# Dense borders by token block, and the loop over two layers written out

## The chip, the cores and the metric

The kernel runs on one core of one Trainium2 chip. The metric is the device time of one execution in microseconds (us); the times given are the median of three runs with their extremes. All inputs and the output are in HBM; the host does no arithmetic.

## The reference

An activation x of 256 tokens by 1024 features (f32) goes through two blocks. The first has two layers, each a mixer (a convolution mixer, then a linear recurrence), a layer norm, a mixture of 16 experts with two chosen per token, and a layer norm. The second, the dense part, has two layers of

```
h = h + 0.5 * swiglu(rms_norm(h, ffn1_norm), w_gate, w_up, w_down)       # 1024 -> 2816 -> 1024
h = h + hybrid_mixer(rms_norm(h, mix_norm), w_in, ..., w_out)           # 1024 -> 3792, attention, 1024 -> 1024
h = h + 0.5 * swiglu(rms_norm(h, ffn2_norm), w_gate, w_up, w_down)
rms_norm(x, g) = x * rsqrt(mean(x*x) + 1e-6) * g
```

The hybrid mixer splits its projection into three kinds of attention (chosen keys, one block, forgetting) with normalised and rotated heads.

## The kernel before

**Layout.** x lies in SBUF as [128 partitions, TB=2 token blocks, 1024]. `xT_hi` and `xT_lo` hold it transposed, [128, KC=8 feature chunks, 256 tokens], cut into a rounded fp32r part and its remainder. Every product of the dense part is made of three fp32r matmuls, hi*hi, hi*lo and lo*hi (`exact`, L1583; `exact_w`, L1891). PSUM has eight banks of 512 f32: `acc` (four: block 0 in banks 0 and 1, block 1 in 2 and 3) collects what is added to x, `W` (four) everything else.

**Weights** come as numbered chunks of up to 128x2048 f32 (1 MB). SyncE's queue loads chunk c into one of six `raw` slots (`load`, L404) once the slot's last chunk has its remainder. ScalarE rounds it to `w_hi` (`split`, L625, one ACTIVATE at L633), VectorE subtracts to `w_lo` (`rest`, L974, one TENSOR_TENSOR at L977); there are three split slots. TensorE waits for `lo_ready` of the chunk and counts `used` when it is done; `split(c)` waits for `used` of chunk c-3. Splits and rests stand in the engines' own order of instructions, written by hand, AHEAD = 3 chunks before TensorE needs them.

**An FFN** (TensorE L1878, ScalarE L864, VectorE L1346) has eleven groups of 256 hidden columns with three chunks each: gate and up (`up`: weights stationary, `xT` moving, 256 tokens wide, 48 matmuls a chunk, into a bank of `W`) and down (`into_acc`, L1610: hidden values stationary, 512 weight columns moving, 24 matmuls a chunk). The groups overlap: gate and up of the next group run before down of this one; an inner loop runs over most groups.

**The mixer** begins with a projection of 16 half chunks (`projection`, L1589: `xT` of a block stationary, 474 weight columns moving, 24 matmuls a chunk, bank by block); its sums are evacuated to `proj`, block 0 by ScalarE (L897), block 1 by VectorE. It ends with `out_projection` (eight chunks of 12 matmuls into `acc`).

**A border** between two stages is: `add_to_x` on VectorE (L1334) waits for the last chunk's `used`, adds `acc` to x for both blocks and signals `x_ready`. `rms` (ScalarE L850, VectorE L1325): ScalarE squares block 0 with a sum, VectorE block 1, ScalarE takes the root of both (L856), VectorE the reciprocal, and each writes its block normalised to `xn` (L858, L1332). `transposes` (TensorE, L1559): eight 128x128 transposes of block 0, then of block 1, into `W`, two feature chunks of both blocks to a bank. `transposed` (ScalarE L643, VectorE L997): eight ACTIVATEs of 128x256 with the norm's gain write `xT_hi`, eight SCALAR_TENSOR_TENSORs write `xT_lo`. VectorE issues the rests of the next chunks between `rms` and `transposed`. Then TensorE starts on the first chunk, waiting pair by pair for `xT_lo` (`wait_xT`).

The dense part stands in a loop over the two layers on every engine (`Fori(0, DEPTH)`, L524, L604, L952, L1535, L2010), so the layer's gain columns and semaphore counts are taken from registers. After it SyncE stores x whole (L534).

## Time and profile before

| | us |
|---|---|
| median of 3 runs (lowest, highest) | 2483.45 (2482.26, 2487.23) |
| the profiled execution | 2489.44 |
| its span, first to last instruction | 2487.8 |
| TensorE busy | 2232.2 (90%) |
| VectorE busy | 955.8 (38%) |
| ScalarE busy | 719.6 (29%) |
| mean granted TensorE clock | 0.942 |

Engines are called PE (TensorE matmul), PEld (TensorE weight load), DVE (VectorE), ACT (ScalarE), POOL (GpSimd), SP (SyncE); a q behind the name is the engine's sequencer or DMA queue. L12 is line 12 of the kernel. Matmuls are pipelined: the duration of one is longer than the distance at which they follow one another, and it is the distance of two starts that tells the pace. The dense part begins at 1233.8 us of the span.

### The profile page before, as it was taken

How to read it: one execution, taken by the hardware profiler on the slowest of the kernel's cores; microseconds unless marked ns; L12 is line 12 of the kernel's file. 1: busy time of each engine (PE TensorE's matmuls, PEld its weight loads, DVE VectorE, ACT ScalarE, POOL GpSimd, SP SyncE). 2: the span in 40 equal slices, each digit the busy share in tenths (PEclk: the TensorE clock that was granted, in tenths of full speed). 3: DMA queues.
4: the chain of work that ended last, by engine and by line, in shares of the span. 5: the costliest groups of instructions: out<-in, count | busy, mean ns of one | idle time of the engine just before them, and what ended most of it. 6: DMA issues, size and time to landing. Idle time of an engine off the chain costs nothing.

```text
span 2487.8 us, 30159 instructions
## 1 busy us (share of the span) xinstructions
PE 2232.2 (90%) x12373; PEld 1559.5 (63%) x12373; DVE 955.8 (38%) x1217; ACT 719.6 (29%) x896; POOL 68.1 (3%) x78
## 2 busy tenths in 40 slices
PE   8869999997866999999599987979989998897998
PEld 6544334332754343333299976769979997676998
DVE  4741000001673000000345557645545546754554
ACT  4621000001451000000333344243343334424332
POOL 2000000000000000000100010000000001000000
PEclk9979999999987999999899989789999999968999
DMA  7189999999439999999955542045545554304551
GB/s 258 37 361 423 425 424 424 423 425 417 163 126 383 425 424 424 424 424 425 333 190 185 177 133 94 1 139 186 185 136 187 186 178 141 101 1 136 176 183 64
DMA packets 194676, 618.56 MB, mean 249 GB/s; under 512 B 10360, under 2 KB 119040, under 8 KB 145408
## 3 DMA queue, kind: packets, MB, share of 16 engines
q1 hardware_dynamic: 192416, 612.01, 64.6%
q0 software_dynamic: 2144, 4.94, 0.8%
q8 instruction: 81, 1.33, 0.2%
q14 instruction: 35, 0.29, 0.0%
HBM read 615.86 MB, written 1.05 MB: 248 GB/s over the span
## 4 chain that ended last, share of the span: by engine, by line
PE 72%; DMA 12%; DVE 8%; ACT 3%; DVEq 2%; issue 2%; ACTq 0%; SPq 0%
PE W L1730 18%; PE W L1892 7%; PE W L1893 7%; PE W L1894 7%; DMA moe_own<-in_moe_w 5%; DMA moe_split<-in_moe_w 5%; PE acc L1620 4%; PE acc L1621 4%; PE acc L1624 4%; PE W L1585 4%; PE W L1586 4%; PE W L1587 4%; PE W L1714 2%; DMA moe_xt<-in_moe_w 2%; PE acc L1723 2%
## 5 line engine op out<-in xcount | busy, mean ns | idle before, releaser
L977 DVE TENSOR_TENSOR w_lo<-raw,w_hi 128x2048 fp32r<-128x2048 f32 (+2 forms) x216 | 466.6, 2163 | 473.4 <-ACT w_hi L633 472.0
L633 ACT ACTIVATE w_hi<-raw 128x2048 fp32r<-128x2048 f32 (+2 forms) x216 | 382.3, 1772 | 595.6 <-PE W L1894 320.6
L1892 PE MATMUL W<-xT_hi,w_hi 128*128 128x256 f32 x1408 | 401.2, 285 | 7.5 <-DVE xT_lo L997 7.5
L1893 PE MATMUL W<-xT_lo,w_hi 128*128 128x256 f32 x1408 | 400.6, 285 | 0.0
L1894 PE MATMUL W<-xT_hi,w_lo 128*128 128x256 f32 x1408 | 400.5, 284 | 0.0
L1228 DVE TENSOR_TENSOR hid<-W,hid 128x512 f32<-128x512 f32 x32 | 22.1, 692 | 735.6 <-PE W L1730 735.6
L1892 PEld LDWEIGHTS W<-xT_hi,w_hi 128*128 128x128 f32 x1408 | 270.2, 192 | 10.3 <-DVE xT_lo L997 8.9
L1893 PEld LDWEIGHTS W<-xT_lo,w_hi 128*128 128x128 f32 x1408 | 270.2, 192 | 1.6
L1894 PEld LDWEIGHTS W<-xT_hi,w_lo 128*128 128x128 f32 x1408 | 270.3, 192 | 0.0
L1585 PE MATMUL W<-w_hi,xT_hi 128*128 128x474 f32 (+1 forms) x400 | 155.3, 388 | 9.9 <-DVE w_lo L977 4.8
L1730 PE MATMUL W<-moe_split,xe 128*64 128x512 f32 x672 | 153.2, 597 | 9.5 <-DMA moe_split<-in_moe_w 8.2
L1586 PE MATMUL W<-w_lo,xT_hi 128*128 128x474 f32 (+1 forms) x400 | 155.3, 388 | 0.0
L1587 PE MATMUL W<-w_hi,xT_lo 128*128 128x474 f32 (+1 forms) x400 | 154.5, 386 | 0.0
L1730 PE MATMUL W<-moe_own,xe 128*64 128x512 f32 x608 | 138.1, 596 | 6.0 <-DMA moe_own<-in_moe_w 5.9
L1620 PE MATMUL acc<-w_hi,hT_hi 128*128 128x512 f32 x352 | 138.3, 393 | 1.7 <-DVEq L1358 1.7
L1730 PE MATMUL W<-raw,xe 128*64 128x512 f32 x576 | 132.1, 597 | 6.9 <-DMA raw<-in_moe_w 6.6
L1621 PE MATMUL acc<-w_lo,hT_hi 128*128 128x512 f32 x352 | 137.7, 391 | 0.0
L1730 PEld LDWEIGHTS W<-moe_split,xe 128*64 128x64 f32 x672 | 45.8, 137 | 112.0 <-issue 90.9
L1624 PE MATMUL acc<-w_hi,hT_lo 128*128 128x512 f32 x352 | 109.3, 392 | 0.0
L1730 PEld LDWEIGHTS W<-moe_own,xe 128*64 128x64 f32 x608 | 41.5, 137 | 99.0 <-issue 77.4
L756 ACT ACTIVATE xe<-W 128x512 f32<-128x512 f32 x32 | 19.1, 597 | 278.3 <-PE W L1714 278.3
L1730 PEld LDWEIGHTS W<-raw,xe 128*64 128x64 f32 x576 | 39.0, 136 | 96.3 <-issue 77.0
(334 smaller groups left out, 2743.9 us busy)
## 6 DMA issues: line engine op xcount, KB each, us to landing
moe_own<-in_moe_w SPq DMA_DIRECT2D x120, 1024.0 KB, 26.2
moe_split<-in_moe_w SPq DMA_DIRECT2D x120, 1024.0 KB, 26.2
raw<-in_moe_w SPq DMA_DIRECT2D x108, 1024.0 KB, 25.8
raw<-in_ffn_w_gate SPq DMA_DIRECT2D x44, 1024.0 KB, 5.3
raw<-in_ffn_w_up SPq DMA_DIRECT2D x44, 1024.0 KB, 5.3
raw<-in_ffn_w_down SPq DMA_DIRECT2D x44, 1024.0 KB, 4.9
moe_xt<-in_moe_w SPq DMA_DIRECT2D x36, 1024.0 KB, 26.0
raw<-in_w_in SPq DMA_DIRECT2D x32, 948.0 KB, 4.9
```

The source lines that it names most:

```text
L633: s.activation(w_hi[split_slot(c)][:, 0:cols], raw[slot_of(c)][:, 0:cols], ACT.Copy).then_inc(hi_ready, 1)
L977: v.tensor_tensor(w_lo[split_slot(c)][:, 0:cols], raw[slot_of(c)][:, 0:cols], w_hi[split_slot(c)][:, 0:cols].bitcast(F32), ALU.subtract).t ...
L1585: t.matmul(out, a_hi, b_hi, start=first, stop=False)
L1586: t.matmul(out, a_hi, b_lo, start=False, stop=False)
L1587: return t.matmul(out, a_lo, b_hi, start=False, stop=last)
L1620: t.matmul(acc[:, 2 * b + n, :], a_hi(k)[:, tok], hi[:, cols], start=st, stop=False)
L1621: t.matmul(acc[:, 2 * b + n, :], a_hi(k)[:, tok], lo[:, cols], start=False, stop=False)
L1624: last = t.matmul(acc[:, 2 * b + n, :], a_lo(k)[:, tok], hi[:, cols], start=False, stop=sp_)
L1730: last = t.matmul(W[CAP * n:CAP * (n + 1), bank, :], stationary[:, kc, :], weights[:, at0 + 512 * n:at0 + 512 * (n + 1)], start=(kc == 0), ...
L1892: t.matmul(out, hi, xT_hi[:, kc, :], start=(kc == 0), stop=False)
L1893: t.matmul(out, hi, xT_lo[:, kc, :], start=False, stop=False)
L1894: return t.matmul(out, lo, xT_hi[:, kc, :], start=False, stop=(kc == KC - 1))
```

## The change

- The three dense loops are written out in Python: addresses and counts are constants. The test for a crowded expert in SyncE's queue stands in layer 0 alone.
- The last chunk into `acc` is computed block by block and signals `acc0` when block 0 is complete. VectorE adds block 0 then (`add_first`), block 1 after the chunk, in two halves (`add_second`).
- Transposes are by block and go to separate banks: block 0 to `W`, block 1 to `acc` (`turned_block`). Copies and remainders are 128 tokens wide, sixteen of each a border.
- Before the mixer x is transposed without its normalisation, which is put as a scale on the evacuations of the projection; block 0's transposes stand inside the last down chunk, block 1's inside the projection's first chunk, whose two halves are computed by block.
- Before an FFN `rms` goes by block, and the two first chunks are computed by block, 128 tokens wide (`up_block`).
- Splits and rests of the next chunks stand at other places around the borders. The output is stored in two halves.

The core of the diff ("..." where lines are left out):

```diff
+        def turned_block(b, kc):
+
+            return (W, acc)[b][:, kc // 2, P * (kc % 2):P * (kc % 2 + 1)]
@@ sync
+            rows_out = out.rearrange("a (b p) d -> p (a b) d", p=P)
+            sp.wait_ge(rm["x0"], 1 + 3 * DEPTH)
+            sp.dma_start(rows_out[:, 0, :], x[:, 0, :]).then_inc(stored, 16)
             sp.wait_ge(x_ready, X_LAYERS + 3 * DEPTH)
-
-            sp.dma_start(out.rearrange("a (b p) d -> p (a b) d", p=P), x[:]).then_inc(stored, 16)
-            sp.wait_ge(stored, 16)
+            sp.dma_start(rows_out[:, 1, :], x[:, 1, :]).then_inc(stored, 16)
+            sp.wait_ge(stored, 32)
 
@@ scalar
+            def turned(call, gain, b, pairs=range(4)):
+
+                for q in pairs:
+                    act.wait_ge(xt_ps, turned_already(call) + 4 * b + q + 1)
+                    for kc in (2 * q, 2 * q + 1):
+                        last = s.activation(xT_hi[:, kc, b * P:(b + 1) * P], turned_block(b, kc), ACT.Copy, scale=gain(kc))
                     last.then_inc(xt_hi_s, 1)
...
+            def rms(call, at0, gain):
+
+                own = slice(0, 512)
+                s.activation(std[:, 0:1], onec[:], ACT.Sqrt)
+                act.wait_ge(rm["x0"], (call + 1).v)
+                s.activation(xn[:, 0, own], x[:, 0, own], ACT.Square, scale=D ** -0.5, accum_out=squares[:, 0:1])
+                act.drain()
+                act.wait_ge(rm["ssd"], at0.times(2).v + 1)
+                s.activation(std[:, 0:1], squares[:, 0:1], ACT.Sqrt, bias=squares[:, 1:2]).then_inc(rm["std"], 1)
+                act.wait_ge(rm["rs"], root_count(call))
+                s.activation(xn[:, 0, :], x[:, 0, :], ACT.Copy, scale=rstd[:, 0:1]).then_inc(rm["xa"], 1)
+                act.wait_ge(rm["x1a"], (call + 1).v)
+                s.activation(xn[:, 1, own], x[:, 1, own], ACT.Square, scale=D ** -0.5, accum_out=squares[:, 2:3])
+                act.drain()
+                xt = N(4 + 4 * (call.base // 3) + (0, 1, 3)[call.base % 3])
+                turned(xt, gain, 0, range(2))
+                act.wait_ge(rm["ssd"], at0.times(2).v + 2)
+                s.activation(std[:, 1:2], squares[:, 2:3], ACT.Sqrt, bias=squares[:, 3:4]).then_inc(rm["std"], 1)
+                turned(xt, gain, 0, range(2, 4))
+                turned(xt, gain, 1)
+
+            def mean_squares(call):
 
                 act.wait_ge(x_ready, (call + X_LAYERS).v)
-                s.activation(xn[:, 0, :], x[:, 0, :], ACT.Square, accum_out=std[:, 0:1])
-                act.drain().then_inc(rm["ssa"], 1)
-                act.wait_ge(rm["ssd"], (call + 1).v)
-                s.activation(std[:], std[:], ACT.Sqrt, bias=rmeps[:], scale=1.0 / D).then_inc(rm["std"], 1)
-                act.wait_ge(rm["rs"], (call + 1).v)
-                s.activation(xn[:, 0, :], x[:, 0, :], ACT.Copy, scale=rstd[:, 0:1]).then_inc(rm["xa"], 1)
...
@@ scalar, mixer
+                        act.wait_ge(rm["rs"], root_count(N(1, (l, 3))))
                     s.activation(proj[:, 0, IN_COLS * j:IN_COLS * (j + 1)], W[:, (2 * j) % 4, 0:IN_COLS],
-                                 ACT.Copy).then_inc(tm_act, 1)
+                                 ACT.Copy, scale=rstd[:, 0:1]).then_inc(tm_act, 1)
...
@@ scalar, loop
-            with act.Fori(0, DEPTH) as l:
+            for l in range(DEPTH):
                 c0 = N(C_LAYERS).plus(l, LAYER_CHUNKS)
-                rms(N(0, (l, 3)))
-                transposed(N(4, (l, 4)), gain_of("ffn1_norm_2", l))
+                rms(N(0, (l, 3)), N(0, (l, 2)), gain_of("ffn1_norm_2", l))
+                split(c0 + (AHEAD - 1))
                 ffn(c0 + C_FFN1, False)
-                rms(N(1, (l, 3)))
-                transposed(N(5, (l, 4)), gain_of("mix_norm_2", l))
+                for b in range(TB):
+                    turned(N(5, (l, 4)), gain_of("mix_norm_2", l), b)
+                split(c0 + (C_FFN1 + FF_CHUNKS - 1 + AHEAD))
+                mean_squares(N(1, (l, 3)))
                 mixer(l, c0)
-                rms(N(2, (l, 3)))
-                transposed(N(7, (l, 4)), gain_of("ffn2_norm_2", l))
+                rms(N(2, (l, 3)), N(1, (l, 2)), gain_of("ffn2_norm_2", l))
+                split(c0 + (C_MIX_OUT + KC - 1 + AHEAD))
                 ffn(c0 + C_FFN2, True)
-                with act.If(l < DEPTH - 1):
-                    for k in range(AHEAD):
+                if l < DEPTH - 1:
+                    for k in range(AHEAD - 1):
...
@@ vector
+            def add_first(call, scale):
+
+                dve.wait_ge(rm["acc0"], call.v)
+                v.scalar_tensor_tensor(x[:, 0, :], acc[:, 0:2, :].rearrange("p a n -> p (a n)"), scale, x[:, 0, :], ALU.mult, ALU.add)
+                v.drain().then_inc(rm["x0"], 1)
+
+            def add_second(count, scale):
+
+                dve.wait_ge(used, count.v)
+                v.scalar_tensor_tensor(x[:, 1, 0:512], acc[:, 2, :], scale, x[:, 1, 0:512], ALU.mult, ALU.add)
+                v.drain().then_inc(rm["x1a"], 1)
+                v.scalar_tensor_tensor(x[:, 1, 512:], acc[:, 3, :], scale, x[:, 1, 512:], ALU.mult, ALU.add)
+                v.drain().then_inc(x_ready, 1)
+            def square_half(b):
+                v.tensor_tensor_reduce(xn[:, b, 512:], x[:, b, 512:], x[:, b, 512:], 1.0 / D, RMS_EPS, ALU.mult, ALU.add,
+                                       squares[:, 2 * b + 1:2 * b + 2])
                 v.drain().then_inc(rm["ssd"], 1)
-                dve.wait_ge(rm["std"], (call + 1).v)
-                v.reciprocal(rstd[:], std[:])
+
+            def reciprocal_root(count, blocks):
+                dve.wait_ge(rm["std"], count)
+                v.reciprocal(rstd[:, blocks], std[:, blocks])
                 v.drain().then_inc(rm["rs"], 1)
+
+            def rms(call, gain, second=None, between=None):
+
+                if second is None:
+                    dve.wait_ge(x_ready, (call + X_LAYERS).v)
+                square_half(0)
+                reciprocal_root(root_count(call), slice(0, 1))
+                if second is not None:
+                    second()
+                square_half(1)
+                xt = N(4 + 4 * (call.base // 3) + (0, 1, 3)[call.base % 3])
+                turned(xt, gain, 0, range(1))
+                reciprocal_root(root_count(call) + 1, slice(1, 2))
                 v.tensor_scalar(xn[:, 1, :], x[:, 1, :], rstd[:, 1:2], None, ALU.mult).then_inc(rm["xd"], 1)
...
+                if between is not None:
+                    between()
+                turned(xt, gain, 0, range(1, 4))
+                turned(xt, gain, 1)
...
@@ vector, loop
-            with dve.Fori(0, DEPTH) as l:
+
+            for l in range(DEPTH):
                 c0 = N(C_LAYERS).plus(l, LAYER_CHUNKS)
-                rms(N(0, (l, 3)))
-                rest(c0)
+                if l == 0:
+                    rms(N(0), gain_of("ffn1_norm_2", l), between=lambda: rest(c0))
                 rest(c0 + 1)
-                transposed(N(4, (l, 4)), gain_of("ffn1_norm_2", l))
                 rest(c0 + 2)
                 ffn(c0 + C_FFN1, N(0, (l, 2 * FF_GROUPS)), False)
-                rms(N(1, (l, 3)))
+
+                add_first(N(1, (l, 3)), 0.5)
+                turned(N(5, (l, 4)), gain_of("mix_norm_2", l), 0)
+                add_second(c0 + (C_FFN1 + FF_CHUNKS), 0.5)
+                turned(N(5, (l, 4)), gain_of("mix_norm_2", l), 1)
                 rest(c0 + (C_FFN1 + FF_CHUNKS - 1 + AHEAD))
-                transposed(N(5, (l, 4)), gain_of("mix_norm_2", l))
+                reciprocal_root(root_count(N(1, (l, 3))), slice(0, TB))
                 mixer(l, c0)
-                rms(N(2, (l, 3)))
+
+                add_first(N(2, (l, 3)), 1.0)
+                rms(N(2, (l, 3)), gain_of("ffn2_norm_2", l), lambda: add_second(c0 + (C_MIX_OUT + KC), 1.0))
+                rest(c0 + (C_MIX_OUT + KC - 2 + AHEAD))
                 rest(c0 + (C_MIX_OUT + KC - 1 + AHEAD))
-                transposed(N(7, (l, 4)), gain_of("ffn2_norm_2", l))
                 ffn(c0 + C_FFN2, N(FF_GROUPS, (l, 2 * FF_GROUPS)), True)
+
+                if l < DEPTH - 1:
+                    rest(c0 + LAYER_CHUNKS)
+                add_first(N(3, (l, 3)), 0.5)
+                if l < DEPTH - 1:
+                    rms(N(3, (l, 3)), gain_of("ffn1_norm_2", l + 1), lambda: add_second(c0 + LAYER_CHUNKS, 0.5))
+                else:
+                    add_second(c0 + LAYER_CHUNKS, 0.5)
 
 
...
@@ tensor
+            def turn_block(call, b, src, ready):
+
+                pe.wait_ge(*ready)
+                for q in range(4):
+                    for kc in (2 * q, 2 * q + 1):
+                        last = t.transpose(turned_block(b, kc), src[:, b, kc * P:(kc + 1) * P], ident[:])
+                    last.then_inc(xt_ps, 1)
+
+            def wait_block(call, b, kc):
+                if kc % 2 == 0:
+                    pe.wait_ge(xt_lo_s, turned_already(call) + 4 * b + kc // 2 + 1)
...
+                if second is not None:
+                    def block(half, b):
+                        c = c0 + half
+                        pe.wait_ge(lo_ready, (c + 1).v)
+                        hi, lo = w_hi[split_slot(c)], w_lo[split_slot(c)]
+                        for k in range(4):
+                            kc = 4 * half + k
+                            wait_block(call, b, kc)
+                            tok = slice(b * P, (b + 1) * P)
+                            last = exact(W[:, b, 0:n], xT_hi[:, kc, tok], xT_lo[:, kc, tok],
+                                         hi[:, k * n:(k + 1) * n], lo[:, k * n:(k + 1) * n], kc == 0, kc == KC - 1)
+                        return last
+
+                    block(0, 0)
+                    second()
+                    block(1, 0)
+                    block(0, 1).then_inc(used, 1)
+                    block(1, 1).then_inc(used, 1)
+                for j in range(0 if second is None else 1, groups):
                     for half in range(2):
...
+                steps = [(k, b) for b in range(TB) for k in range(kn)] if final else [(k, b) for k in range(kn) for b in range(TB)]
...
+                    if ends and (k, b) == (kn - 1, 0):
+                        last.then_inc(rm["acc0"], 1)
+                    if midway is not None and (k, b) == (0, 1):
+                        midway()
                 last.then_inc(used, 1)
...
+                def up_block(c, bank, b):
+
+                    pe.wait_ge(lo_ready, (c + 1).v)
+                    hi, lo = w_hi[split_slot(c)], w_lo[split_slot(c)]
+                    for f in range(2):
+                        for kc in range(KC):
+                            if f == 0:
+                                wait_block(call, b, kc)
+                            cols = slice(kc * FF_COLS + f * P, kc * FF_COLS + (f + 1) * P)
+                            last = exact_w(W[:, bank, f * SEQ + b * P:f * SEQ + (b + 1) * P], hi[:, cols], lo[:, cols], kc,
+                                           slice(b * P, (b + 1) * P))
+                    return last
+
+                def exact_w(out, hi, lo, kc, tok=slice(0, SEQ)):
...
-                up(c0 + 1, 1)
+                    into_acc(c, 2, lambda k: hT_hi[:, parity, k, :], lambda k: hT_lo[:, parity, k, :], first, final, final, midway)
+
+                turn_block(call, 0, xn, (rm["xa"], norm_count))
+                up_block(c0, 0, 0)
+                turn_block(call, 1, xn, (rm["xd"], norm_count))
+                up_block(c0 + 1, 1, 0)
+                up_block(c0, 0, 1).then_inc(used, 1)
+                up_block(c0 + 1, 1, 1).then_inc(used, 1)
```

## Rows read from the trace of the kernel before

**Rows 1.** The page's chain of work that ended last, shares by engine.
```profile
PE 72%; DMA 12%; DVE 8%; ACT 3%; DVEq 2%; issue 2%; ACTq 0%; SPq 0%
```

**Rows 2.** Timeline of VectorE, FFN1 to mixer, layer 0: start, duration (us), instruction [idle before].
```profile
1433.84 2.35 DVE L1338 SCALAR_TENSOR_TENSOR x<-acc,x 128x1024 f32<-128x1024 f32 x2 [2.38 <-PE acc L1624]
...
1444.45 3.28 DVE L997 SCALAR_TENSOR_TENSOR xT_lo<-W,vecs,xT_hi 128x256 fp32r<-128x256 f32 x8 [1.73 <-ACT xT_hi L643]
```

**Rows 3.** Timeline of ScalarE, the same border.
```profile
1437.85 1.28 ACT L856 ACT_TABLE_LOAD   x1 [0.45 <-issue]
...
1439.70 1.15 ACT L858 ACTIVATE xn<-x,rstd 128x1024 f32<-128x1024 f32 x1 [0.26 <-DVEq L1331]
1443.45 3.03 ACT L643 ACTIVATE xT_hi<-W,vecs 128x256 fp32r<-128x256 f32 x8 [2.60 <-PE W L1564]
```

**Rows 4.** Timeline of TensorE's matmuls, the same border.
```profile
1440.90 3.68 PE L1564 MATMUL W<-ident,xn 128*128 128x128 f32 x16 [7.11 <-ACT xn L858]
1446.21 0.76 PE L1585 MATMUL W<-w_hi,xT_hi 128*128 128x474 f32 x1 [1.63 <-DVE xT_lo L997]
...
1449.14 0.60 PE L1586 MATMUL W<-w_lo,xT_hi 128*128 128x474 f32 x1
...
1451.02 0.38 PE L1587 MATMUL W<-w_hi,xT_lo 128*128 128x474 f32 x1
...
1451.87 0.38 PE L1585 MATMUL W<-w_hi,xT_hi 128*128 128x474 f32 x1
```

**Rows 5.** Timeline of ScalarE: rows at which a border begins or its first chunks end.
```profile
1233.81 1.06 ACT L853 ACTIVATE xn<-x 128x1024 f32<-128x1024 f32 x1 [1.18 <-DVEq L1046]
...
1257.10 1.91 ACT L633 ACTIVATE w_hi<-raw 128x2048 fp32r<-128x2048 f32 x1 [1.94 <-PE W L1894]
...
1654.27 1.91 ACT L633 ACTIVATE w_hi<-raw 128x2048 fp32r<-128x2048 f32 x1 [0.80 <-PE acc L1624]
...
1681.28 1.91 ACT L633 ACTIVATE w_hi<-raw 128x2048 fp32r<-128x2048 f32 x1 [1.93 <-PE W L1894]
...
1883.22 1.91 ACT L633 ACTIVATE w_hi<-raw 128x2048 fp32r<-128x2048 f32 x1 [1.94 <-PE W L1894]
...
2059.95 1.91 ACT L633 ACTIVATE w_hi<-raw 128x2048 fp32r<-128x2048 f32 x1 [4.71 <-PE acc L1624]
...
2082.99 0.57 ACT L897 ACTIVATE proj<-W 128x474 f32<-128x474 f32 x1 [3.40 <-PE W L1587]
...
2305.39 1.91 ACT L633 ACTIVATE w_hi<-raw 128x2048 fp32r<-128x2048 f32 x1 [1.93 <-PE W L1894]
```

**Rows 6.** Timeline of VectorE: mixer to FFN2, then FFN2 to FFN1.
```profile
1653.50 2.29 DVE L977 TENSOR_TENSOR w_lo<-raw,w_hi 128x2048 fp32r<-128x2048 f32 x1 [0.43 <-ACT w_hi L633]
...
1856.89 2.36 DVE L1338 SCALAR_TENSOR_TENSOR x<-acc,x 128x1024 f32<-128x1024 f32 x2 [8.91 <-PE acc L1624]
1862.70 1.22 DVE L1327 CUSTOM_DVE_ANT_0 xn<-x 128x1024 f32<-128x1024 f32 x1 [3.45 <-issue]
```

**Rows 7.** Timeline of all engines: loads and matmuls as an FFN starts.
```profile
1871.40 0.19 PEld L1892 LDWEIGHTS W<-xT_hi,w_hi 128*128 128x128 f32 x1 [2.37 <-DVE xT_lo L997]
...
1871.51 0.19 PEld L1893 LDWEIGHTS W<-xT_lo,w_hi 128*128 128x128 f32 x1
1871.63 0.28 PE L1893 MATMUL W<-xT_lo,w_hi 128*128 128x256 f32 x1
...
1871.98 0.28 PE L1893 MATMUL W<-xT_lo,w_hi 128*128 128x256 f32 x1
```

**Rows 8.** Timeline of weight loads: the router's, 16 columns of fp32r.
```profile
156.23 0.10 PEld L1585 LDWEIGHTS W<-xT_hi,wr_hi 128*16 128x16 f32 x1 [1.19 <-issue]
156.26 0.10 PEld L1586 LDWEIGHTS W<-xT_lo,wr_hi 128*16 128x16 f32 x1
```

**Rows 9.** The chain in order of time: four f32 matmuls of 128 columns.
```profile
1582.44 0.85 PE W L1976 x4
```

**Rows 10.** Timeline: the final store is issued.
```profile
2483.42 0.39 SPq L534 DMA_DIRECT2D out<-x  x1
```

More of the change, by code:

```diff
@@ L110, in __init__ @@
     def __init__(self, base, *terms):
-        self.base, self.terms = base, terms
+        self.base = base + sum(r * k for r, k in terms if isinstance(r, int))
+        self.terms = tuple((r, k) for r, k in terms if not isinstance(r, int))
     def __add__(self, n):
@@ L192, in build_program @@
         std = at("std", [P, TB])
+        squares = at("squares", [P, 4])
         rstd = at("rstd", [P, TB])
@@ L477, in first_after_moe @@
                 def first_after_moe(i):
-                    if which == 1:
+                    if which == 1 and l == 0:
                         sp.wait_ge(moe_used, raw_freed(1, i))
@@ L499, in ffn @@
                     down(c + 2, j)
-                    if j == 0 and which == 1:
-                        more_rounds(1, crowded(sp, 1, l))
+                    if j == 0 and which == 1 and l == 0:
+                        more_rounds(1, crowded(sp, 1))
                     if j == 0:
@@ L672, in layer_norm @@
                 if c_next is not None:
-                    split(N(c_next + 1), after_moe=i // 2)
-                    split(N(c_next + 2), after_moe=i // 2)
+                    for k in range(1, AHEAD - 1 if c_next == C_LAYERS else AHEAD):
+                        split(N(c_next + k), after_moe=i // 2)
             transposed(N(0))
@@ L887, in ffn @@
                             silu(1 - t, c0 + (i + 1))
-                if not last:
-                    split(c0 + (FF_CHUNKS - 1 + AHEAD))
             def mixer(l, c0):
@@ L2007, in mixer @@
                 wait_xT(N(6, (l, 4)))
[L2008 to L2010 removed]
+                out_projection(c0 + C_MIX_OUT, ends=True)
+            for l in range(DEPTH):
                 c0 = N(C_LAYERS).plus(l, LAYER_CHUNKS)
[L2013 to L2018 removed]
+                ffn(c0 + C_FFN1, N(0, (l, 2 * FF_GROUPS)), N(4, (l, 4)), 2 * l + 1,
+                    lambda: turn_block(N(5, (l, 4)), 0, x, (rm["x0"], N(2, (l, 3)).v)))
                 mixer(l, c0)
[L2020 to L2021 removed]
+                ffn(c0 + C_FFN2, N(FF_GROUPS, (l, 2 * FF_GROUPS)), N(7, (l, 4)), 2 * l + 2)
 SMALL_LOADS = 4 + sum(len(names) for names in VEC_SETS)
```

143 lines of the change are left out of this document (65 added, 78 removed).

## The prediction

> **What bounds the kernel now.** I read the chain of waits first. TensorE is 72% of it, DMA 12%, VectorE 8% and ScalarE 3% [rows 1]. The DMA share lies in the mixture of experts, which the change leaves alone; the VectorE and ScalarE share is to be looked for between the dense stages. The timelines of one border (the first FFN's end to the mixer's start, layer 0) show it: addition to x, squares, root, normalisation, 16 transposes, eight gained copies and eight remainders, and TensorE standing from about 1433.8 to 1446.2 but for the transposes [rows 2 to 4]. There are six borders into a norm (norm to FFN1, FFN1 to mixer, mixer to FFN2, FFN2 to FFN1, FFN1 to mixer, mixer to FFN2) and the end. Inside the FFNs TensorE takes each chunk without a pause, so what a border gains or loses reaches the end whole.
>
> To compare, I take for each border the moment E, at which the last product is done, and the moment at which the work that the change reorders (the two first chunks) is used up. ScalarE's rows that wait for that moment give it [rows 5]: norm to FFN1 1233.8 to 1257.1, 23.3 us; mixer to FFN2 1654.3 (its last split starts there) to 1681.3, 27.0 (the second layer's end, 2305.39, is 624 later, as its whole border is); FFN2 to FFN1 1856.9 [rows 6] to 1883.2, 26.3; FFN1 to mixer 2060.0 to 2083.0, 23.0 (in layer 0 TensorE's first eight or so matmuls start 0.4 us apart, later ones 0.2125, (1451.87-1451.02)/4 [rows 4]: half rate, 1.2 for 2.4 GHz, some 1.6 more).
>
> **Borders into the mixer.** The final down product now ends block 0 after 12 of its 24 matmuls, 2.74 us before E. Call that A. VectorE adds block 0 in 1.2 (half of L1338's 2.35 [rows 2]). TensorE has one six-matmul step of block 1 meanwhile, so it waits some 0.5, transposes block 0 (half of 3.68 cold [rows 4], near 1.0 warm by its 16 at half that) and then has the last step, 1.4, as cover. An activation of 128 columns I put at 0.27 us: 256 take 0.38 (3.03/8), 1024 take 1.15 [rows 3]. A remainder of 128 is 0.28 by 3.28/8 and 1.18 [rows 2]. A pair is thus 0.55 on either engine, where it was 0.8; the doubled count costs little. Block 0 is ready at about A+4.7, but its first half, which is all that half a chunk needs, at A+3.6. The products start at A+4.3. Four pieces of 12 matmuls at 0.2125 [rows 4] are 2.6 each. Behind the first piece TensorE waits for x of block 1: VectorE does it after block 0's remainders, two halves of 0.7, at A+6.5, just in time; transposes 1.2; then the second piece covers block 1's copies. End at about A+16, or E+13.3, where it was E+23.0. The moved rest of the third chunk (2.3 [rows 6]) ends near A+13.8 and TensorE asks for it at A+16; mean_squares (two squares, 2.4, and the table load of 1.28 [rows 3]) ends its reciprocal near A+15.9 and is asked for with the first evacuation. Both are hidden; without that cover they would cost about 2 each. The normalisation itself, which was on the path, has gone into the evacuation's scale at no cost. **Gain 9.7 in layer 1, 11.3 in layer 0: 21 us.**
>
> **Borders into an FFN: the price of a matmul of 128 columns.** Here up_block halves the moving columns (256 to 128) and doubles the count: 192 matmuls and 192 weight loads where 96 were. No fp32r matmul of under 256 columns is in the trace. What bounds it? At 1871.40 an empty TensorE starts a load; the next load starts 0.11 later, and the second matmul 0.23 later, the following at 0.117 each [rows 7]. So a load of 128x128 fp32r holds its path for 0.11, and behind it a 256-column matmul for as long again. With weights of 16 columns two loads start 0.03 apart [rows 8]: the 0.11 goes with the number of weight columns, and halving the moving columns doesn't touch it. Bounds: from below 0.060, half of today's spacing, if columns alone set it; from above 0.213, as 128-column matmuls of f32 are spaced (0.85/4) [rows 9], if narrow fp32r falls back to that. I take 0.113, between the 0.11 of a load and the 0.117 at which pairs with the same load run [rows 7], the nearest in kind. Then the two chunks cost 21.7 us of TensorE instead of 11.5: +10.2 at each of four borders.
>
> **What they win.** FFN2 to FFN1, from E: acc0 comes 2.74 before it, x of block 0 at -1.4. Squares of half a row on each engine (half of L1327's 1.22 [rows 6]), root with its table loaded ahead (1.28 hidden [rows 3]), reciprocal: +0.25; the copy of block 0, 1.15: xn0 at +1.5, where the transposes started at +8.9. Writing the loop out also takes away the 3.4 that VectorE stood without a releaser at the turn of the loop [rows 6], all within that 8.9. But then one pair after another comes, held up on VectorE by reciprocal and xn1 (0.17+0.75): the fourth remainder ends at +6.5, the first block's two halves at +10.5, block 1's transposes at +11.6.
>
> **The new wait.** up_block(c0+1, 1, 0) waits for lo_ready of the second chunk. Before, both rests stood ahead of the remainders. Now VectorE issues rest(c0+1) behind all of turned(..., 1), which needs ScalarE's copies of block 1, which need the transposes that TensorE issues just before this wait. In its queue nothing can pass. Last pair +13.9 (four pairs, 2.2, behind the transposes), rest 2.3: TensorE goes on at +16.3, having stood 4.6. Three pieces of 48 at 0.113 follow, 16.3, and signals: +33.3 against 26.3. **Loss 7.** SyncE's loads wait for these rests too, but the FFN asks for a megabyte in 5.8 us and has six slots: hidden.
>
> Mixer to FFN2: block 0 has only a six-matmul lead (1.4), and ScalarE's table load falls after its last split. xn0 at +3.7, fourth remainder +8.7, block 0's piece +12 to 13.5, transposes, stall, +19; pieces and a little half-rate running: +36 against 27. Loss 9, twice. To its credit the rest that delayed the addition (1653.50 to 1655.8 [rows 6]) stands behind it now; that is in these numbers. Norm to FFN1: nothing of x is ready early. The rest of the first chunk, 2.3, is put between xn1 and the remainders, so the fourth is ready at +10.2 after x; +13.6 (warm) to 17.5 (half rate) for the piece, transposes and stall +19.5 to 23, end +36 to 40 against 23.3. Loss 14. **FFN borders: -7-9-9-14 = -39.** Running at half rate after a wait, as the first matmuls of layer 0's mixer do [rows 4], is where these four vary by 2 or 3 each.
>
> **The end.** x of block 1 in halves is ready 0.8 sooner; of the final store (issued 2483.42, the span ends at 2487.8 [rows 10]) half goes ahead, and 0.5 MB at the 2.6 us that 1 MB moves is 1.3 less: 2 us.
>
> **Sum:** 21 + 2 - 39 = 16 us slower. The profiled execution took 2489.4 (span 2487.8), 6.0 above the median of 2483.45; so 2505.5 in its terms and **2499.5** in the median's. Other edits (fixed instead of register addresses, squares, the SyncE test left out) I put at nothing, within 1 either way: they lie beside running matmuls, except that 16 small instructions could be quicker with fixed scalars.
>
> **Rivals.**
> A, the other side: the moving columns set the pace, and the load hides behind the stream before it. Then a matmul takes 0.067 (0.060 and an allowance), and 168 of the 192 at each border (the first 24 wait for remainders anyway) are 0.046 cheaper, 31 us in all: 2468. It decides from a spacing of about 0.09 down. For it: the stream at 256 columns doesn't slow with 128-column weights against 16. Against: the 0.11 between loads [rows 7, 8]. Chance 0.19.
> B: narrow fp32r runs as f32, 0.213 per matmul: 0.1 more on 168 at four borders, 67 us: 2566. Nothing here shows or excludes it. 0.12.
> C: the load spacing holds, but the stall is smaller, since the rest lands before TensorE gets there (it would have to overtake the remainders), or the small copies are quicker: four stalls of 4.6 off: 2481. Against it is the written order. 0.09.
> D: something between A and my value. The Trainium skill, TensorE: Matmul & The Clock Gate, "Back-to-back issue gap", gives load and matmul pairs of 128 columns a sustained 81 ns. By it the 168 would be 0.032 cheaper each, 21.5 us in all, which gives 2478. The trace has no such pair; its loads 0.11 apart speak against it. From rows the same place is the middle of 0.060 and 0.113 (0.087): 2482. Chance 0.07.
>
> **Chances.** My forecast 0.53, its own range 2489 to 2512. Measurement tells this kernel from no change at about 0.2%, 5 us, thus 2478.5 to 2488.4. Faster: A 0.19, half of D 0.04, a third of C 0.03: 0.26. Same: 0.03 of D and 0.05 of C: 0.08. Slower: forecast 0.53, B 0.12, the rest of C: 0.66. The range takes in A and leaves out most of B: 2464 to 2520.
>
> **What would show it.** The distance of two up_block matmuls at full clock: 0.11, 0.065 or 0.21. TensorE's idle before block (c0+1, 0) in each FFN, released by w_lo: 4 to 5 us, four times. At the mixer borders no idle above 1 us, and the time from E to the first evacuation near 13. If the spacing is 0.11 and the total is faster, my reckoning of the gaps is wrong; if the spacing is less, the price was.

## The result: slower by 3.9%, and where it went

The changed kernel takes 2583.11 us (median of four runs, 2582.44 to 2585.31); the kernel before, run beside it, 2485.34. The ratio is 1.0391, with a 95% interval of 1.0372 to 1.0409. The forecast was 2499.5 in a range of 2464 to 2520: the sign was right, the time lies far outside. The profiled execution took 2582.44 with a span of 2580.4, 92.6 more than the span before, and its mean granted clock was 0.920 where it was 0.942.

The chain of waits, answering to [rows 1], and the granted clock in 40 slices, from the page of the changed kernel:

```profile
PEclk9979999998979999999599997969987999887899
...
PE 73%; DMA 13%; DVE 8%; ACT 3%; DVEq 2%; issue 1%; ACTq 0%; SPq 0%
```

The chain's shares say next to nothing: TensorE has a point more. The clock line says more: the dense half, from the 20th digit on, holds a 5, a 6 and three 7s where it held a 6 and a 7, though TensorE's share of busy time has risen to 91%. ScalarE's rows that wait for the moment at which the two first chunks are used up, or for the mixer's first sums, answer to [rows 5]:

```profile
1242.07 0.63 ACT L877 ACTIVATE xn<-x 128x512 f32<-128x512 f32 x1 [4.19 <-DVEq L1092]
...
1297.40 1.91 ACT L653 ACTIVATE w_hi<-raw 128x2048 fp32r<-128x2048 f32 x1 [6.42 <-PE W L2025]
...
1490.36 0.64 ACT L937 ACTIVATE proj<-W,rstd 128x474 f32<-128x474 f32 x1
...
1732.40 1.91 ACT L653 ACTIVATE w_hi<-raw 128x2048 fp32r<-128x2048 f32 x1 [6.42 <-PE W L2025]
...
1960.94 1.91 ACT L653 ACTIVATE w_hi<-raw 128x2048 fp32r<-128x2048 f32 x1 [6.42 <-PE W L2025]
...
2153.30 0.64 ACT L937 ACTIVATE proj<-W,rstd 128x474 f32<-128x474 f32 x1
...
2398.00 1.91 ACT L653 ACTIVATE w_hi<-raw 128x2048 fp32r<-128x2048 f32 x1 [6.42 <-PE W L2025]
```

The difference of neighbouring rows is the length of a stretch; each holds one border and the undisturbed work around it. Set against the same stretches of before (layer 0's first evacuation was at 1458.56 there), in us; the last column is the version with whole chunks of the next section:

| stretch | before | changed | difference | predicted | whole chunks, difference |
|---|---|---|---|---|---|
| up to x ready | 1233.8 | 1242.1 | +8.3 | 0 | +8.7 |
| norm to FFN1 | 23.3 | 55.3 | +32.0 | +14 | +0.7 |
| to the mixer, layer 0 | 201.5 | 193.0 | -8.5 | -11.3 | -10.3 |
| to FFN2, layer 0 | 222.7 | 242.0 | +19.3 | +9 | -10.8 |
| FFN2 to FFN1 | 201.9 | 228.5 | +26.6 | +7 | -6.2 |
| to the mixer, layer 1 | 199.8 | 192.4 | -7.4 | -9.7 | -8.6 |
| to FFN2, layer 1 | 222.4 | 244.7 | +22.3 | +9 | -11.3 |
| to the end | 182.4 | 182.4 | 0.0 | -2 | -1.2 |

In what follows a matmul is narrow with 128 moving columns and wide with 256, and the level is the granted clock: 0.50 is half (1.2 GHz), 1.00 is full (2.4 GHz). The four borders into an FFN cost 100.2, not 39, and something ahead of the dense part costs 8.3. One FFN border in windows (columns: window, its length, busy time and instructions of TensorE, its weight loads, VectorE, ScalarE and GpSimd, granted clock, DMA share, GB/s):

```profile
1250.00:1260.00 10.00, 9.74 (x46) 9.74 (x46) 1.76 (x7) 0.00 (x0) 0.00 (x0) 0.50 0.36 107
1262.00:1266.00 4.00, 0.49 (x3) 0.09 (x1) 4.00 (x9) 3.22 (x7) 0.00 (x0) 0.50 0.00 0
1266.00:1276.00 10.00, 9.68 (x46) 9.69 (x46) 2.46 (x2) 0.00 (x0) 0.00 (x0) 0.50 0.62 210
1276.00:1297.00 21.00, 21.00 (x100) 21.00 (x100) 2.29 (x1) 3.79 (x3) 0.00 (x0) 0.50 0.17 51
1297.00:1303.00 6.00, 6.00 (x36) 6.00 (x36) 3.46 (x4) 1.91 (x1) 0.00 (x0) 0.65 0.01 5
```

The second window is the new wait. After it TensorE stands no more, and yet the granted clock stays at 0.50 for all 144 narrow matmuls that follow, 0.213 us each (the 100 of the fourth window include those that overlap its edges). Only among the wide matmuls that come then does it rise, at 1301.2, after 19 of them; at the other three borders it is 12 or 13. The new wait did not take the clock. At all four borders the level was at 0.50 before it, from 1232.9, 1683.5, 1915.6 and 2349.1 on, behind the earlier waits for x, xn or the first remainders, and at 0.50 it stayed until 1301.2, 1734.7, 1963.4 and 2400.3. The rows of the border FFN2 to FFN1 show both prices side by side:

```profile
1913.76 0.30 PE L2023 MATMUL W<-xT_hi,w_hi 128*128 128x128 f32 x1 [1.39 <-DVE xT_lo L1042]
1913.90 0.27 PE L2024 MATMUL W<-xT_lo,w_hi 128*128 128x128 f32 x1
1914.01 0.28 PE L2025 MATMUL W<-xT_hi,w_lo 128*128 128x128 f32 x1
1914.12 0.28 PE L2023 MATMUL W<-xT_hi,w_hi 128*128 128x128 f32 x1
...
1915.31 0.33 PE L2023 MATMUL W<-xT_hi,w_hi 128*128 128x128 f32 x1 [0.69 <-DVE xT_lo L1042]
...
1915.78 0.42 PE L2023 MATMUL W<-xT_hi,w_hi 128*128 128x128 f32 x1
1915.99 0.41 PE L2024 MATMUL W<-xT_lo,w_hi 128*128 128x128 f32 x1
```

Starts 0.11 apart while the clock is still full, as forecast; 0.21 apart once it has fallen. The stall is as large as forecast too, 3.83 us here against 4.6:

```profile
1266.32 0.47 PE L2023 MATMUL W<-xT_hi,w_hi 128*128 128x128 f32 x1 [3.83 <-DVE w_lo L1019]
```

The mixer's border, answering to [rows 2 to 4], first TensorE, then VectorE:

```profile
1475.75 1.09 PE L1673 MATMUL W<-ident,x 128*128 128x128 f32 x8 [0.34 <-DVEq L1377]
...
1480.67 1.04 PE L1673 MATMUL acc<-ident,x 128*128 128x128 f32 x8
```
```profile
1474.45 1.22 DVE L1376 SCALAR_TENSOR_TENSOR x<-acc,x 128x1024 f32<-128x1024 f32 x1
1476.88 2.16 DVE L1042 SCALAR_TENSOR_TENSOR xT_lo<-W,vecs,xT_hi 128x128 fp32r<-128x128 f32 x8 [1.22 <-ACT xT_hi L666]
1478.96 0.68 DVE L1382 SCALAR_TENSOR_TENSOR x<-acc,x 128x512 f32<-128x512 f32 x1
...
1485.10 2.29 DVE L1019 TENSOR_TENSOR w_lo<-raw,w_hi 128x2048 fp32r<-128x2048 f32 x1 [1.19 <-ACT w_hi L653]
1488.81 0.17 DVE L1394 RECIPROCAL rstd<-std 128x2 f32<-128x2 f32 x1 [1.42 <-ACT std L899]
```

From the first addition (1474.45) to the first evacuation (1490.36) is 15.9 us, where the prediction had 16 from its point A, and TensorE's one idle gap here is 0.34. Both groups of transposes ran at the full clock (1.09 and 1.04 for eight), and it never fell at this border.

### The profile page after: what moved, and what is told of

The parts are those of the page before. It is cut to its first block, busy times and chain, and to the rows that moved or that the text cites. A ratio compares the mean times of both kernels' runs of the same rounds, so it can differ in the third digit from the quotient of the medians.

```text
span 2580.4 us, 30299 instructions
## 1 busy us (share of the span) xinstructions
PE 2343.1 (91%) x12757; PEld 1665.7 (65%) x12757; DVE 959.8 (37%) x1277; ACT 724.7 (28%) x959; POOL 69.7 (3%) x78
## 4 chain that ended last, share of the span: by engine, by line
PE 73%; DMA 13%; DVE 8%; ACT 3%; DVEq 2%; issue 1%; ACTq 0%; SPq 0%
PE W L1850 17%; PE W L2023 8%; PE W L2025 8%; PE W L2024 8%; DMA raw<-in_moe_w 4%; DMA moe_split<-in_moe_w 4%; DMA moe_own<-in_moe_w 4%; PE acc L1736 4%; PE acc L1735 4%; PE acc L1739 4%; PE W L1682 4%; PE W L1683 4%; PE W L1684 4%; PE W L1834 2%; PE acc L1843 1%
## 5 line engine op out<-in xcount | busy, mean ns | idle before, releaser
L2023 PE MATMUL W<-xT_hi,w_hi 128*128 128x256 f32 (+1 forms) x1536 | 471.5, 307 | 22.0 <-DVE w_lo L1019 18.7
L2024 PE MATMUL W<-xT_lo,w_hi 128*128 128x256 f32 (+1 forms) x1536 | 470.2, 306 | 0.0
L2025 PE MATMUL W<-xT_hi,w_lo 128*128 128x256 f32 (+1 forms) x1536 | 470.1, 306 | 0.0
L2023 PEld LDWEIGHTS W<-xT_hi,w_hi 128*128 128x128 f32 x1536 | 332.6, 217 | 27.1 <-DVE w_lo L1019 20.7
L2024 PEld LDWEIGHTS W<-xT_lo,w_hi 128*128 128x128 f32 x1536 | 332.7, 217 | 1.7
L2025 PEld LDWEIGHTS W<-xT_hi,w_lo 128*128 128x128 f32 x1536 | 332.7, 217 | 0.0
```

The lines of the kernel that those rows point to most:

```text
L2023: t.matmul(out, hi, xT_hi[:, kc, tok], start=(kc == 0), stop=False)
L2024: t.matmul(out, hi, xT_lo[:, kc, tok], start=False, stop=False)
L2025: return t.matmul(out, lo, xT_hi[:, kc, tok], start=False, stop=(kc == KC - 1))
```

## The experiments

All are edits of the changed kernel or of the kernel before; none leaves work out, several add some. In the diffs "..." stands for lines left out.

**1. The two first FFN chunks whole.** Everything else of the change stays.

```diff
+                            if first and f == 0:
+                                wait_block(call, 1, kc)
...
                 turn_block(call, 0, xn, (rm["xa"], norm_count))
-                up_block(c0, 0, 0)
                 turn_block(call, 1, xn, (rm["xd"], norm_count))
-                up_block(c0 + 1, 1, 0)
-                up_block(c0, 0, 1).then_inc(used, 1)
-                up_block(c0 + 1, 1, 1).then_inc(used, 1)
+                up(c0, 0, True)
+                up(c0 + 1, 1)
```

> The changed kernel, but the two first chunks of each FFN are computed whole (256 tokens a matmul, as before), behind the transposes of both blocks; all else as changed. Theory 1 (a matmul of 128 columns is bound by its weight load, 0.11 us at full clock, and a stream of such matmuls leaves the clock at 1.2 GHz, so 0.213): 41 us of narrow matmuls and a stall go at each of four borders, and what is left of the change is its gain: about 2443, at most 2455. Theory 2 (narrow fp32r runs as f32): the same time. The theory that the waits of the new order cost the time and the width little: above 2520.

Measured: 2449.37 (2447.22 to 2454.63), 0.9857 of before (0.9834 to 0.9880), 134 less than the changed kernel. The last column of the table shows it by stretch: all borders but the first gain 6 to 11. The clock was down here as well behind the transposes, at all four borders (rows of TensorE at the first):

```profile
1256.45 0.41 PE L2026 MATMUL W<-xT_lo,w_hi 128*128 128x256 f32 x1
1256.67 0.41 PE L2027 MATMUL W<-xT_hi,w_lo 128*128 128x256 f32 x1
1256.88 0.31 PE L2025 MATMUL W<-xT_hi,w_hi 128*128 128x256 f32 x1
1257.03 0.28 PE L2026 MATMUL W<-xT_lo,w_hi 128*128 128x256 f32 x1
1257.15 0.29 PE L2027 MATMUL W<-xT_hi,w_lo 128*128 128x256 f32 x1
```

Wide matmuls start at 0.21 and go to 0.12 after 19 of them; at the other borders after 16, 6 and 10. So the block-wise chunks, with the wait that they bring, are the loss; the rest of the change is worth some 36.

**2. A filler.** One matmul of 256 columns on the tile of zeros beside three narrow ones, into a free bank, to see whether denser work lifts the clock.

```diff
+                            if bank == 1 or b == 1 or f == 1 or kc >= 6:
+                                t.matmul(W[:, 3, 0:SEQ], zeros[:], hi[:, 0:SEQ], start=True, stop=True, skip_group_check=True)
```

> The changed kernel with work added: beside each three matmuls of 128 columns one more of 256 columns on zero weights into a free bank (58 in each FFN), result unused. Theory 1: the clock rises to 2.4 GHz in this stretch, narrow matmuls follow at 0.113 and the fillers at 0.12; 41 us become some 29 at each of four borders, and the chunks behind start at full rate: about 50 us faster than the changed kernel, 2530. Theory 2: nothing is won and the fillers cost 0.12 to 0.21 each: 28 to 50 us slower, 2610 to 2635.

Measured (two runs, as in experiments 3 and 4): 2635.52, 1.0604 (1.0577 to 1.0631). The clock stayed at 0.50 from 1276 to 1314. The 58 fillers of a border at 0.213 are 12.4, four times 49, and 52.4 were added. A quarter of wide work on zeros doesn't lift the clock; whether the zeros matter was not told apart.

**3. Narrow matmuls inside the running FFN.** The kernel before, its third group's gate and up in two halves of 128 tokens.

```diff
-                            last = exact_w(W[:, bank, f * SEQ:(f + 1) * SEQ], hi[:, cols], lo[:, cols], kc)
...
+                                last = exact_w(W[:, bank, f * SEQ + at0:f * SEQ + at0 + width], hi[:, cols], lo[:, cols], kc,
+                                               slice(at0, at0 + width))
...
-                group(c0 + 5, 1, h0 + 2, False)
+                group(c0 + 5, 1, h0 + 2, False, (128, 128))
```

> The kernel before; only in the third group of each FFN, in the middle of a stream at full clock, gate and up are computed in two halves of 128 tokens: 192 matmuls where 96 were, no wait or pause near them. Theory 1: the first ones follow at 0.11 to 0.12, then the granted clock falls to half and the others at 0.213: +20 to +28 us per FFN, 2565 to 2600 in all. Theory 2: 0.213 from the first on while the clock is granted full. The rival that pauses, not the width, took the clock: 0.113 throughout, +10 us per FFN, 2525.

Measured: 2519.04, 1.0136 (1.0112 to 1.0159). Rows and a window of TensorE:

```profile
1271.98 0.28 PE L1898 MATMUL W<-xT_hi,w_lo 128*128 128x128 f32 x1
...
1273.21 0.28 PE L1897 MATMUL W<-xT_lo,w_hi 128*128 128x128 f32 x1
```
```profile
1272.00:1286.00 14.00, 14.00 (x128) 14.00 (x128) 4.35 (x3) 4.31 (x3) 0.00 (x0) 1.00 0.45 149
```

Eleven steps in 1.23 are 0.1118 each, at clock 1.00 throughout. This throws out rival B (narrow fp32r as slow as f32) and rival A (columns set the pace); 0.113 was the price. The time is nearest to the rival's 2525. And this narrow stream, which begins at the full level, stays there. By the Trainium skill, TensorE: Matmul & The Clock Gate, "Back-to-back issue gap", the pace would be 0.081; these rows say 0.112 for fp32r.

**4. The wait taken away.** The rest of the second chunk stands between block 0's and block 1's remainders (`ahead` is that rest, handed to `rms` at each of the borders).

```diff
                 turned(xt, gain, 0, range(1, 4))
+                ahead()
                 turned(xt, gain, 1)
```

> The changed kernel, with one edit: VectorE issues the rest of the second chunk of each FFN between the remainders of block 0 and those of block 1, so TensorE's wait of 3.8 to 4.2 us for it goes. Theory 1: four waits shrink to the one for the first remainders of block 1 (about 1.5), so 9 to 16 us faster than changed, 2567 to 2574; the narrow matmuls stay at 0.213. The rival that the pause is what keeps the clock low: the clock comes up, and 60 us or more go, below 2525.

Measured: 2534.91, 1.0200 (1.0175 to 1.0225), so 48 less, where the waits themselves are 15: between the two expectations. At the borders norm to FFN1 and FFN2 to FFN1 the clock rose behind block 1's transposes; at the two from a mixer it did not (windows of the first and of the second border):

```profile
1266.00:1278.00 12.00, 12.00 (x110) 12.00 (x109) 3.01 (x2) 3.80 (x3) 0.00 (x0) 1.00 0.28 89
1674.00:1709.00 35.00, 35.00 (x167) 35.00 (x166) 6.75 (x10) 7.77 (x12) 0.00 (x0) 0.50 0.25 85
```

The same instructions, about 0.11 us each in one place and 0.21 in the other (12.00/110 and 35.00/167, a little low since a window also counts the matmuls at its edges). The theory that came of it: pauses drop the clock, and a narrow stream keeps whichever level it meets.

**5 and 6. A burst in the wait.** 32 matmuls on real data between block 1's transposes and the wait, 256 columns wide in one kernel, 128 in the other.

```diff
                 turn_block(call, 1, xn, (rm["xd"], norm_count))
+                for _ in range(32):
+                    t.matmul(W[:, 3, 0:256], xT_hi[:, 0, 0:P], w_hi[split_slot(c0)][:, 0:256], start=True, stop=True,
+                             skip_group_check=True)
                 up_block(c0 + 1, 1, 0)
```

> The changed kernel, with 32 more matmuls of 256 moving columns on real data (xT_hi of block 0 stationary, the first 256 columns of the first chunk moving, into a free bank) between block 1's transposes and the wait for the second chunk's rest, at all four borders into an FFN. At the half clock they take 32 x 0.213 = 6.8 us, 3.8 of it in the stall: +3 a border, +12 in all. Theory 1 (a narrow stream holds the level at which it starts, a wide one raises it): the clock is full behind the burst, the 144 narrow matmuls behind it follow at 0.113 instead of 0.213, 14.4 us a border or 58 in all: 2583 + 12 - 58 = 2537. Theory 2 (the clock stays low for a time that the pause sets, whatever runs): low until the same moment as before, 2583 + 12 = 2595.

Measured: 2522.99, 1.0143 (1.0127 to 1.0158): 60 less than without the burst, though work was added, and 14 less than expected. The level was full within the burst at all four borders. It isn't a time that the pause sets. It rose after 8, 14, 3 and 15 matmuls of the burst, and eight transposes stand right ahead of it, so this run alone doesn't tell what raised it.

> As the kernel with the wide burst, but the 32 added matmuls have 128 moving columns: same count, same loads, same 0.213 us apart at the half clock, so same 6.8 us. Theory 1 (width raises the clock): it stays low, 2583 + 12 = 2595, pace 0.213 behind the burst. Rival (it is the uninterrupted stream over the stall that raises it, whatever its width): as with the wide burst, 2537.

Measured: the profiled execution took 2522.81 and showed the level up at all four borders; its other executions took 2520.06, 2556.05 and 2719.22 (the last at a mean granted clock of 0.805, where the profiled one had 0.948), so no median of it is used. Its windows, the transposes, then the burst:

```profile
1261.60:1263.20 1.60, 1.60 (x10) 1.60 (x10) 0.17 (x1) 0.83 (x4) 0.00 (x0) 0.50 0.00 0
1263.20:1264.60 1.40, 1.40 (x9) 1.40 (x9) 1.40 (x7) 1.40 (x7) 0.00 (x0) 0.55 0.00 0
1264.60:1267.00 2.40, 2.40 (x24) 2.40 (x23) 2.40 (x4) 1.75 (x1) 0.00 (x0) 1.00 0.00 0
```

My expectation fell: there a narrow burst was enough, and the level rose after 6, 7, 1 and 2 of its matmuls. Either an unbroken stream does it whatever its width, or the transposes just before (f32, 128 columns too, 0.213 apart at the half level) did, and the burst only kept the wait from undoing it. The next three tell that.

**7 and 8. The same bursts away from the transposes**, between the second and the third narrow piece, where TensorE has no pause on either side.

> The changed kernel with 32 matmuls of 256 moving columns on real data between the second and the third of the four narrow pieces, behind the stall and away from the transposes. Theory W (a wide stream raises the clock where the narrow one doesn't): full level within the burst, so the two last pieces follow at 0.113 instead of 0.213 (9.6 us less a border), the wide matmuls behind them start at full rate (3.5 less), and the burst costs 5.5: 2583 + 4 x (5.5 - 9.6 - 3.5) = 2553. Theory T (it is raised only by the transposes with a stream right behind them, without the stall): stays low, 2583 + 4 x 6.8 = 2610.

> As the one with the late wide burst, but the 32 added matmuls have 128 moving columns, 0.213 apart at the half level as all others. Theory W: stays low, 2583 + 4 x 6.8 = 2610. Theory T: the same, 2610. Rival (a stream on one repeated weight tile raises the clock whatever its width, which would also explain the burst over the stall): as with the wide burst, 2553.

Measured: wide 2563.35, 1.0309 (1.0293 to 1.0325); narrow 2609.35, 1.0495 (1.0475 to 1.0515). The windows with and behind the burst, wide first:

```profile
1275.00:1278.00 3.00, 3.00 (x16) 3.00 (x16) 0.00 (x0) 0.00 (x0) 0.00 (x0) 0.50 0.00 0
1278.00:1281.00 3.00, 3.00 (x20) 3.00 (x20) 0.00 (x0) 0.00 (x0) 0.00 (x0) 0.68 0.00 0
1281.00:1284.00 3.00, 3.00 (x29) 3.00 (x29) 0.00 (x0) 0.00 (x0) 0.00 (x0) 1.00 0.02 5
```
```profile
1276.00:1283.50 7.50, 7.50 (x37) 7.50 (x37) 0.00 (x0) 0.00 (x0) 0.00 (x0) 0.50 0.01 2
1283.50:1304.00 20.50, 20.50 (x98) 20.50 (x98) 2.29 (x1) 3.80 (x3) 0.00 (x0) 0.50 0.17 51
```

Same count, same loads, same 0.213 at the half level, TensorE busy without a break in both: the wide burst lifts the clock at four borders of four (after 22, 11, 23 and 12 of its matmuls), the narrow one at none. The wide one is 20 below the changed kernel but 10 above its 2553; the 10 were not traced. At this place the two kernels differ in nothing but the width, so it is shown here that 32 wide matmuls bring the clock back and 32 narrow ones don't. It isn't width alone everywhere: experiments 4, 6 and 9 have rises with nothing wide near. What the chip counts stays open.

**9. Eight transposes at that place.**

```diff
                 up_block(c0 + 1, 1, 0)
+                for k in range(8):
+                    t.transpose(W[:, 3, 0:P], xn[:, 0, k * P:(k + 1) * P], ident[:])
```

> The changed kernel with eight more 128x128 transposes (f32, of block 0's xn into a free bank) where the late bursts stood, between the second and the third narrow piece; 0.24 us apart at the half level, so 2 us a border. Theory T (eight transposes with an unbroken narrow stream on both sides raise the clock, which is what happened when a narrow burst filled the stall behind block 1's transposes): full level shortly behind them, 2583 + 4 x (1.7 - 9.6 - 3.5) = 2537. Theory W (only a longer stretch of wide work does it, and the narrow burst over the stall was helped by something else): stays low, 2583 + 4 x 2 = 2591.

Measured: 2571.23, 1.0335 (1.0316 to 1.0353), between the two. Windows behind them at the four borders:

```profile
1278.00:1299.00 21.00, 21.00 (x101) 21.00 (x100) 2.29 (x1) 3.79 (x3) 0.00 (x0) 0.50 0.16 51
1720.00:1731.00 11.00, 11.00 (x96) 11.00 (x94) 2.29 (x1) 3.80 (x3) 0.00 (x0) 0.95 0.01 1
1940.00:1960.00 20.00, 20.00 (x96) 20.00 (x95) 2.29 (x1) 3.79 (x3) 0.00 (x0) 0.50 0.17 53
2379.00:2390.00 11.00, 11.00 (x97) 11.00 (x95) 2.29 (x1) 3.80 (x3) 0.00 (x0) 0.96 0.01 1
```

Neither theory as stated: the transposes lift the clock at two of four, after 6 and 5 of the narrow matmuls behind them. That agrees with two of four in experiment 4 (after 7 and 4). With experiment 6 it is 8 places of 12 where eight transposes ran into a narrow stream without a pause: the level rose within 7 matmuls or not until wide ones came. In the changed kernel, where the new wait follows them, it is none of four. The trace of the kernel before shows the same helper: its sixteen transposes in a row, at the half level when they began, were followed by the full level at three of the four borders into an FFN (here FFN2 to FFN1; transposes from 1865.76 to 1869.4, wide matmuls from 1871.40):

```profile
1866.00:1869.00 3.00, 3.00 (x15) 3.00 (x15) 3.00 (x2) 0.69 (x2) 0.00 (x0) 0.50 0.10 11
1870.00:1871.00 1.00, 0.00 (x0) 0.00 (x0) 1.00 (x4) 1.00 (x4) 0.00 (x0) 1.00 1.07 381
```

For experiment 6 this makes the transposes the likely helper; why it is some borders and not others, and that kernel's spread of times, were not explained.

**10. The 8 us ahead of the dense part.** The change puts a tile `squares` of 16 bytes (32 with rounding) ahead of rstd, which moves all tiles behind it. The kernel before with nothing but such a gap:

```diff
         std = at("std", [P, TB])
+        pad = at("pad", [P, 4])
         rstd = at("rstd", [P, TB])
```

> The kernel before with one unused tile of 16 bytes (32 with rounding) ahead of rstd in SBUF, where the change has its tile squares; no instruction differs but in addresses. Theory 1: the shift by 32 bytes slows the mixture of experts (its loads land in tiles behind it) and is why the dense part begins 8 us late in all versions of the change: x ready at 1242, 2485 + 8 = 2493. Theory 2: the place of the tiles does nothing and the 8 us come from another edit (the SyncE queue's written-out loop, the test left out for layer 1): 2485 within 2.

Measured: 2497.44 (2494.70 to 2500.22), 1.0043 (1.0029 to 1.0056). The DMA issues of the mixture of experts, kernel before first (count, KB each, us from issue to landing):

```profile
moe_own<-in_moe_w SPq DMA_DIRECT2D x120, 1024.0 KB, 26.2
...
raw<-in_moe_w SPq DMA_DIRECT2D x108, 1024.0 KB, 25.8
```
```profile
moe_own<-in_moe_w SPq DMA_DIRECT2D x120, 1024.0 KB, 26.4
...
raw<-in_moe_w SPq DMA_DIRECT2D x108, 1024.0 KB, 26.4
```

x is ready at 1243.81, 10.0 later than before. In the window 850 to 1100 the DMAs move 421 GB/s with the gap and 424 without. Over the roughly 900 us in which the page shows this rate that is 6 us, an estimate; the rest was not traced. Of the places that these loads fill only the six `moe_own` tiles lie behind the gap; `raw` lies ahead of it and hasn't moved, and yet its loads take 26.4 for 25.8.

**11. The gap made 64 bytes**, in the version with whole chunks.

> The changed kernel with its two first FFN chunks whole, and the tile squares made 64 bytes instead of 16 (32 with rounding). Theory 1 (the 32-byte shift costs 8 us in the first block): x ready at 1234, 2449 - 8 = 2441. Theory 2 (place does nothing): 2449, x ready at 1242.5.

Measured: 2446.76 (2444.93 to 2448.71), 0.9838 (0.9823 to 0.9854); x ready at 1242.74, still 421 GB/s. The expectation that 64 bytes would cure it fell; the time is 2.6 below experiment 1, and the runs of the two overlap.

**12. No gap**, in the version with whole chunks: squares lies in the unused bytes behind std.

```diff
-        std = at("std", [P, TB])
-        squares = at("squares", [P, 4])
+        roots = at("std", [P, 8])
+        std, squares = roots[:, 0:TB], roots[:, 4:8]
```

> The changed kernel with the two first FFN chunks whole, and squares put into the unused bytes behind std, so that every other tile lies where it lay before the change. Theory (any shift of the tiles behind it slows the transfers of the mixture of experts): x ready at 1233 to 1234 again instead of 1242.5, and 2449 - 8 = 2441. If 64 bytes of shift had cost little and the 8 us came from the instructions of the change, it is 2447 to 2449 as the other two versions with whole chunks.

Measured: 2441.28 (2440.57 to 2444.09), 0.9819 (0.9805 to 0.9832), the fastest of all, 424 GB/s:

```profile
1236.02 0.63 ACT L877 ACTIVATE xn<-x 128x512 f32<-128x512 f32 x1 [4.19 <-DVEq L1092]
```

x is ready 6.5 earlier than in experiment 1, though not at the expected 1233 to 1234. All fourteen traces bear the cause out. The three with the tiles in their old place (before, experiments 3 and 12) move 424 GB/s in this window and have x ready at 1233.2 to 1236.0; the eleven with a shift move 421 and have it at 1240.7 to 1244.9. Only 32 and 64 bytes were tried, and no larger shift; why the address matters stays open.

## Why the prediction was wrong

**The price of a narrow matmul** was right: 0.113 forecast, 0.1118 measured at full clock, 0.213 at half. B's figure came true by another way than B's: not the form of the matmul but the level of the clock.

**The step that failed** is "Running at half rate after a wait, as the first matmuls of layer 0's mixer do [rows 4], is where these four vary by 2 or 3 each". The four losses are 10 to 20 above their forecast (32.0, 19.3, 26.6 and 22.3 for 14, 9, 7 and 9). I took from [rows 4] that the clock comes back after some eight matmuls whatever runs; those were 474 columns wide. Here the level was down before the new wait, and neither the first 48 narrow matmuls nor the 144 behind it brought it back, each 0.1 dearer. The "three pieces of 48 at 0.113", 16.3 in the sum, took 31.1 at each border (from the end of the wait, 1266.3 at the first, to the signal at 1297.4): 14.8 more, 59 of the 61 over the four (100.2 instead of 39). The rest lies ahead of the new wait's end and was not split up. The Trainium skill, TensorE: Matmul & The Clock Gate, Part 1, ties the rise to sustained activity and not to what is issued; the window with 21.00 of 21.00 us busy (by the profile's count) at 0.50 and experiments 7 and 8 disagree.

**The new wait** was there four times, 3.8 us where 4.6 was forecast. Its price was more than its length: without it the kernel is 48 faster (experiment 4), with a burst in its place 60. It didn't bring the clock down; it stood between the transposes and the narrow stream, and where nothing stood there the level came back at 2 borders of 4 (experiment 4) or at 4 of 4 (6).

**The borders into the mixer** were forecast at 21 and gave 18.9 with whole chunks, 15.9 in the changed kernel, where the FFN ahead still starts at half level. The cover for rest and mean_squares held.

**What they win** was misjudged only in size: with whole chunks, FFN2 to FFN1 gains 6.2 and the two mixer-to-FFN2 stretches 10.8 and 11.3, and the first border loses 0.7. Early addition and normalisation pay; the halved chunks cost more than all of it.

**The end**: from the last addition (now 2575.78) to the last instruction is 4.6, it was 6.8: 2.2 less, 2 forecast. The stretch as a whole came out even: with whole chunks it gains 1.2, which the changed kernel loses again by starting it at the half level (until 2400.3). The remaining 1 was not traced.

**Not foreseen at all**: 8.3 from the place of the tiles, shifted by one tile of 16 bytes (6.5 of 8.7 came back when nothing moved; the traces without a shift differ by 2.8 among themselves). The "other edits" that were put at nothing include squares, but as instructions; where its tile lies wasn't thought of. The sum of the misses: 8.3 + 61.2 + 5.1 (mixers) + 2.0 (end) = 76.6, which is 92.6 less the 16 forecast.

## What to carry to other kernels

Cutting a stage's first matmuls narrower to start them sooner is priced by the clock that they meet: in this kernel the narrow ones behind a pause ran at half level to their end, and wide ones took it back within their first chunk. So start early with what is ready, but keep the first matmuls wide, and don't let a narrow stream follow a pause. When a change adds a tile, put it where nothing else moves, and compare the untouched part of the kernel first.

## What was not expected of the hardware

- 128 columns of fp32r with a 128x128 load each: 0.1118 us apart at full clock, 0.213 at half; 256 columns: 0.12 and 0.213. At half level the narrow one costs as much as the wide one, for half the work.
- Full level was kept by a narrow stream (14.00 us at 1.00), and not regained by one (20.50 us at 0.50): the price of the same stream depends on what ran before it.
- In the middle of a narrow stream 32 wide matmuls lifted the level at four borders of four, eight f32 transposes at two of four, 32 narrow ones at none. Right behind eight transposes, without a pause, a narrow burst saw it rise at four of four (the profiled execution of experiment 6).
- 32 or 64 bytes of shift of some of the destination tiles in SBUF: 421 instead of 424 GB/s in all fourteen traces (eleven with, three without).
